# Where split weights lie inside their slots: one fixed place for a form, or sixteen places in turn

## The reference

```
proj = h @ w_in                      # 2048 x 16512, and 2048 x 15376 in the second layer
merged = (jax.nn.sigmoid(ga) * (ya @ w_up_a) + jax.nn.sigmoid(gb) * (yb @ w_up_b)
          + jax.nn.sigmoid(gc) * (yc @ w_up_c))
return x + merged @ w_o
...
x = x + (jax.nn.silu(h2 @ w_ffn_gate[l]) * (h2 @ w_ffn_up[l])) @ w_ffn_down[l]
```

## Time and profile before

| | |
|---|---|
| Median of 2 runs | 2914.48 us (2913.48 to 2915.48) |
| The profiled execution, first to last instruction | 2913.4 us |
| PE busy | 2882.6 us, 99% |
| PE weight loads busy | 2491.1 us, 86% |
| VectorE busy | 1619.3 us, 56% |
| ScalarE busy | 1344.1 us, 46% |
| DMA, mean share of 16 engines | 59% |

### The profile page before, as it was taken

One profiled execution on the slowest core, in us unless ns is written; L12 is line 12 of the kernel. 1 busy time (PEld: TensorE's weight loads), 2 busy tenths in 40 slices (PEclk: granted clock), 3 DMA queues, 4 the chain that ended last, 5 costly groups with the idle time before them and its releaser, 6 DMA issues.

```text
span 2913.4 us, 42709 instructions
## 1 busy us (share of the span) xinstructions
PE 2882.6 (99%) x18228; PEld 2491.1 (86%) x18228; DVE 1619.3 (56%) x1860; ACT 1344.1 (46%) x1533; POOL 73.7 (3%) x173
## 2 busy tenths in 40 slices
PE   7999999999999999999999999999999999999998
PEld 7979888888988888889998899888888888888886
DVE  5565665656656556564555466554654544544444
ACT  5452543544554454454455454444444444444443
POOL 5000000001000000000000000000000000000000
PEclk9999999999999999999999999999999999999999
DMA  7443444566665655566556566666566666666564
GB/s 211 125 143 112 134 128 118 166 195 184 227 194 184 189 163 185 191 188 182 174 161 202 166 174 174 196 194 195 192 184 195 188 193 188 188 189 206 192 194 152
DMA packets 356178, 518.30 MB, mean 178 GB/s; under 512 B 18288, under 2 KB 137220, under 8 KB 355220
## 3 DMA queue, kind: packets, MB, share of 16 engines
q1 hardware_dynamic: 355220, 512.37, 58.7%
q0 software_dynamic: 768, 3.20, 0.4%
HBM read 513.39 MB, written 2.11 MB: 177 GB/s over the span
## 4 chain that ended last, share of the span: by engine, by line
PE 98%; DVE 1%; ACT 0%; DMA 0%; issue 0%; SPq 0%; DVEq 0%; ACTq 0%
PE gp L1668 23%; PE gp L1670 23%; PE gp L1669 23%; PE gp L1677 7%; PE gp L1679 7%; PE gp L1678 7%; PE ps L1845 4%; PE ps L1727 1%; PE ps L1802 1%; PE ps L1833 1%; DMA gain<-in_norm_g 0%; PE ps L1787 0%; PE ps L1823 0%; PE ps L2045 0%; PE ps L2062 0%; PE ps L2053 0%
## 5 line engine op out<-in xcount | busy, mean ns | idle before, releaser
L1058 DVE TENSOR_TENSOR w_lo<-w_raw,w_hi 128x1024 fp32r<-128x1024 f32 (+2 forms) x976 | 1166.2, 1202 | 949.6 <-ACT w_hi L653 944.7
L653 ACT ACTIVATE w_hi<-w_raw 128x1024 fp32r<-128x1024 f32 (+2 forms) x976 | 1011.0, 1041 | 1106.4 <-PE gp L1670 877.7
L1668 PE MATMUL gp<-w_hi,h_hi 128*128 128x512 f32 x2112 | 833.5, 395 | 1.5 <-DVE w_lo L1058 1.5
L1670 PE MATMUL gp<-w_lo,h_hi 128*128 128x512 f32 x2112 | 822.7, 390 | 0.0
L1669 PE MATMUL gp<-w_hi,h_lo 128*128 128x512 f32 x2112 | 822.2, 389 | 0.0
L1677 PE MATMUL gp<-h_hi,w_hi 128*128 128x256 f32 x1696 | 488.4, 288 | 1.8 <-DVE h_lo L1123 1.8
L1678 PE MATMUL gp<-h_lo,w_hi 128*128 128x256 f32 x1696 | 474.5, 280 | 0.0
L1679 PE MATMUL gp<-h_hi,w_lo 128*128 128x256 f32 x1696 | 474.3, 280 | 0.0
L1668 PEld LDWEIGHTS gp<-w_hi,h_hi 128*128 128x128 f32 x2112 | 396.6, 188 | 83.8 <-DVE w_lo L1058 1.9
L1670 PEld LDWEIGHTS gp<-w_lo,h_hi 128*128 128x128 f32 x2112 | 396.5, 188 | 83.3
L1669 PEld LDWEIGHTS gp<-w_hi,h_lo 128*128 128x128 f32 x2112 | 396.8, 188 | 80.5 <-issue 0.5
(11 more groups left out here) (290 smaller groups left out, 1805.3 us busy)
## 6 DMA issues: line engine op xcount, KB each, us to landing
w_raw<-in_w_in SPq DMA_DIRECT2D x384, 512.0 KB, 4.0
w_raw<-in_w_ffn_gate SPq DMA_DIRECT2D x88, 512.0 KB, 4.4
w_raw<-in_w_ffn_up SPq DMA_DIRECT2D x88, 512.0 KB, 4.4
w_raw<-in_w_ffn_down SPq DMA_DIRECT2D x88, 512.0 KB, 4.1
w_raw<-in_w_in SPq DMA_DIRECT2D x136, 256.0 KB, 3.2
w_raw<-in_w_in SPq DMA_DIRECT2D x128, 192.0 KB, 3.1
w_raw<-in_w_mem_kv SPq DMA_DIRECT2D x32, 512.0 KB, 4.3
w_raw<-in_w_o SPq DMA_DIRECT2D x32, 512.0 KB, 4.3
```

Source lines behind the costliest of these rows:

```text
L653: act.activation(in_slot(w_hi, n), w_raw[:, slot, 0:size], ACT.Copy).then_inc(sem("hi_done"), 1)
L1058: dve.tensor_tensor(in_slot(w_lo, n), w_raw[:, slot, 0:size], in_slot(w_hi, n).bitcast(F32), ALU.subtract)\
L1668: pe.matmul(o, xh, wh, start=(k == 0), stop=False)
L1670: ins = pe.matmul(o, xh, wl, start=False, stop=(k == last_k))
```

## The change

A block's floats no longer lie at a place set by its form. The blocks of each form are counted, and the n-th one lies at `4 * (n % 16)` floats, which is 0, 16, 32, ... 240 bytes past the slot's beginning. All units of a block have the same place. Instructions, their order, shapes, DMAs and waits are the same as before. Form `rows` goes through all sixteen places some six times (744 of its 8928 matmuls lie at place 0, and 6456 at places that are no multiple of 64 bytes). The 5088 matmuls of the other forms, with 12, 8, 8 and 2 blocks, use places 0 to 176 bytes (`wide`), 0 to 112 (`pair`, `trio`), and 0 and 16 (`narrow`); 3792 of them are at places that are no multiple of 64 bytes.

```
-SHIFT = {'rows': 0, 'wide': 16, 'pair': 16, 'trio': 16, 'narrow': 16}
+PLACES = 16
...
+    place, of_kind = [], Counter()
+    for b in blocks:
+        place.append(4 * (of_kind[b.kind] % PLACES))
+        of_kind[b.kind] += 1
...
         def in_slot(w, n):
-            at = SHIFT[blocks[units[n][0]].kind]
+            at = place[units[n][0]]
             return w[:, n % RING, at:at + unit_size(n)]
```

## The result

The changed kernel takes 2968.33 us (2967.4 to 2969.26) against 2914.48: 1.0185 times as long, with an interval from 1.0169 to 1.0202. That is 53.9 us, at the upper end of the range on record and just past it. The profiled execution spans 2967.5 us.

What follows compares the result with a forecast made beforehand. The prediction took TensorE's stream of matmuls to bound the kernel: 2913.4 + 11.5 (moving weights) + 4.0 (stationary weights) = 2928.9 us, with the runs' median 1.1 us above that span, so 2930.0 us, +0.5%. Range: 2908 to 2968 us.

Steps and rivals of the forecast that it cites:

- The bound: Whole kernel: TensorE's matmuls follow one another, PE busy 99%, so only the distance between their starts can move the time.
- ScalarE's and VectorE's pass: cost zero: Pass over a unit at new places: even 10% more, 0.23 us a unit, stays beneath TensorE's 2.7 us; cost zero.
- The moving weights of form `rows`, +11.5 us: 8184 `rows` matmuls leave place 0; some lose 4.4 ns meeting weight loads badly: 11.5 us, bounds 0 and 36.0 us.
- the share of 0.32: Part of moved `rows` matmuls taken as slow: half the weight-stationary forms' 0.64, since spare time lets bad meetings heal.
- The stationary weights, +4.0 us: Weight-stationary forms at new distances: half of the way to the slower pace, 117.8 ns; bounds -14.8 and +8.1 us.
- every place but the old ones is bad: Rival: all moved `rows` matmuls at 231.1 ns, all weight-stationary ones at 117.8: +44.1 us, 2959 us; chance 0.11.
- The 24-byte row: Plain fp32 matmul, moving operand 24 bytes past a multiple of 256: 215 ns, so an odd beginning by itself costs nothing.
- No effect: Rival: the two paces depend on when a load and a matmul meet, not on addresses; 2914 us; chance 0.30.
- The 64-byte piece: Rival: TensorE fetches 64-byte pieces, so places off multiples of 64 need one more: +88.5 us, 3003 us; chance 0.07.
- The lost tick regained: Rival: some distance between operands removes the 17/16, `rows` at 213.3 ns: -119 us, 2795 us for all; chance 0.02.
- The repetition every sixteen blocks: Sign in quiet `rows` blocks: distances above 226.7 ns in some and 226.7 in others, repeating every sixteen blocks.
- Loads of 192 ns on the lines of form `rows`: Sign in the profile after: weight loads of 192 ns appear on `rows` lines, where they lasted 188 ns before.

Runs made afterwards that it cites:

- the isolated grid: Program with TensorE alone, form `rows`, 512 columns, all 16x16 pairs of moving and stationary places; at stationary 0 it reproduces the changed kernel's paces; no pair below 226.6 ns.
- rows_scan: Against the kernel before, only form `rows` goes through the sixteen places, other forms stay at 64 bytes: 2954.75 us against 2913.62, 1.0138.
- The grid's line for 256 columns: TensorE alone, 256 moving columns at place 0, stationary at all sixteen places: 113.3 ns at 64 bytes, up to 120.0 ns at others.
- micro_width: TensorE alone, 448 to 128 moving columns at all sixteen places, stationary at 0: spread 6.7 to 7.9 ns at 448 to 320 columns, 111.7 ns at 192 and 128.

## Why the prediction was wrong, step by step

*The bound* was read rightly: only the distances between TensorE's starts moved, and no wait did.

*ScalarE's and VectorE's pass: cost zero.* Right: in form `rows` the means at the sixteen places are 1057 to 1061 ns and 1222 to 1229, and the isolated grid gives the loss without either engine.

*The moving weights of form `rows`, +11.5 us.* This is the step that failed, and by far: 41.1 us when it was changed alone. Two choices in it were off. The price of a bad meeting was taken from the earlier trace rows, 231.1 ns, as if that were the slow state of this form. The places' own paces reach 234.6, and the earlier trace rows is no lasting state at all. It is how a stretch at place 0 begins after an interruption: nine or so uneven distances (229, 234, 236, 224 ns and so on), then 226.7 for as long as it runs. The timeline of the kernel before shows it, the first pair nine matmuls apart, the second thirty:

```profile
203.34 0.39 PE L1669 MATMUL gp<-w_hi,h_lo 128*128 128x512 f32 x1
...
205.42 0.39 PE L1669 MATMUL gp<-w_hi,h_lo 128*128 128x512 f32 x1
...
212.22 0.39 PE L1669 MATMUL gp<-w_hi,h_lo 128*128 128x512 f32 x1
```

2.08 and 6.80 us are 231.1 and 226.7 ns. And the share of 0.32 came from the thought that spare time in the weight loads lets a bad meeting heal. At the new places it doesn't heal: 14 of the 15 are slow through whole blocks. The stretch of the earlier trace rows heals because it lies at place 0, whose lasting pace is 226.7 ns. The isolated grid's first line times the counts of matmuls at each place gives +44.6 us, 5.0 ns for a matmul of form `rows`; the trace of rows_scan has the same 5.0 ns, and the 41.1 us of the run are less by what the other forms gained.

*The stationary weights, +4.0 us* between bounds of -14.8 and +8.1. Measured alone: +12.8, beyond the upper bound. Again the slower of two paces that the trace happened to hold, 117.8 ns, was taken for the worst, and the places run at up to 120. The grid's line for 256 columns times the counts gives +11.0 us.

*The bounds.* The case "every place but the old ones is bad" named the right shape, with a chance of 0.11, and priced it at +44.1 us where it is +53.9. A bound from the nearest rows is a bound only if those rows were made by the thing that changes. Rows 4 and 5 come from one pair of places, and so do rows 6 and 7; none shows a pair that the change brings in.

*The 24-byte row.* Plain fp32 matmuls take twice the time for a column, and at 24 bytes the place costs nothing: 215 ns from start to start, as for the aligned L1860 pair. (The prediction compared the two by their recorded 0.59 us, which is no measure of cost; the starts agree.) I kept that row as evidence for small effects. At one tick a column it says nothing: 24 bytes there has 233.3 ns, and 20 bytes is the worst place of all, 240.0.

*The rivals.* No effect: out, since both operands' places decide the pace. The 64-byte piece: out in its form. It asks for 226.7 ns at 64, 128 and 192 bytes, and these have 229.0, 232.5 and 233.3. A step of 16 ticks does appear, in the time after which a pattern repeats and in a spread that hardly grows with the columns (micro_width), but which address is slow follows no such rule. The lost tick regained: out, no pair of 256 is below 226.6 ns.

*What the profile was to show.* The repetition every sixteen blocks came out, and PE's waits stayed. Loads of 192 ns on the lines of form `rows` came out only in part. In the stretch 1950:2030 us, whose blocks lie at 160 to 224 bytes and run at 231.1 to 234.7 ns, the loads last 188 ns on average, as in the earlier trace rows. In a block at 240 bytes that runs at 236 ns (713:737 us) the mean is 190 to 191 by line, and four in ten are longer than 190. First two lines of the former, then one of the latter:

```profile
L1673 PEld LDWEIGHTS gp<-w_hi,h_hi 128*128 128x128 f32 x99 | 18.6, 188 | 4.6
L1675 PEld LDWEIGHTS gp<-w_lo,h_hi 128*128 128x128 f32 x98 | 18.4, 188 | 4.5
...
L1674 PEld LDWEIGHTS gp<-w_hi,h_lo 128*128 128x128 f32 x32 | 6.1, 191 | 1.3
```

The block at 208 bytes is nearly as slow, 234.7 ns, and has no such loads. So the load's recorded duration is no sure sign of the loss.

*The page weighed against the trace.* The Trainium skill's page "SBUF — State Buffer", section "Specifications (TRN2)", has 16-byte lines, by which, as the prediction reads it, steps of 16 bytes would be free: the runs disagree, with 226.7 against 231.6 ns. The Trainium skill's section "Who interferes with whom" of that page has TensorE never waiting on anyone, with two independent read ports. The runs agree that no other engine takes part, and disagree on the two ports: the stationary place changes the pace of the moving read, 226.7 to 233.3 ns from stationary 0 to 32.

What stays open is why. The pace depends on the places of both operands modulo 256 bytes as far as tried (slots at odd and at even multiples of 256 run alike), a common shift of 32 bytes is free but for a few pairs and one of 16 is not, the places of the neighbouring matmuls count too, and the length of the load changes which places are slow. Where in TensorE or SBUF the two reads meet, and what picks one of two states where a pair has both, was not found.

## What to carry to other kernels

A kernel whose bound is a stream of fp32r matmuls has two hidden parameters, the byte places of the moving and of the stationary read, worth up to 3.5% of a matmul in form `rows` here (226.7 to 234.6 ns) and 6% at 256 columns (113.3 to 120.0). For 512 moving columns align both to 256 bytes: that pair came back to 226.7 ns in all 24 entries. For 256 test pairs in an isolated program, each by many ways in, and then in the kernel. Read such a cost from the distance between starts, never from an instruction's duration. And where a trace holds a resource in one setting only, its states are no bounds for the other settings.

## What the runs showed of the hardware that was not expected

- TensorE alone, at the full granted clock: 512 fp32r columns take 226.7 to 240.0 ns by the places of the two reads, 256 columns 113.3 to 123.3 ns, and a pattern of distances repeats after a multiple of 6.67 ns.
- A pair of places can have two lasting states. 64/64 at 256 columns is at 113.3 or 117.8 ns by how long the plain fp32 matmul before it was (up to 128 columns, 15 of 24 entries, against 136 and more, 9); with the lo part at 192 bytes it is at 113.3 in all 24.
- With 192 or 128 moving columns the moving place is free, at stationary place 0: 111.7 ns everywhere.
- At 512 columns and places (0, 0) a stretch in the kernel before takes five to eleven matmuls after an interruption, at 231.1 ns each in the earlier trace rows, before it runs at 226.7.
- Loading 32 columns instead of 128 doesn't make the moving read faster: 226.7 to 240.0 ns over the sixteen places.
